# Two moves in the last jobs of the first feed-forward: the parameters' copy ahead of the fifth job's settling, and one modulation transfer behind the next weights

## The chip, the cores and the metric

The kernel runs on one core of a Trainium2 chip. The metric is the device time of one execution in microseconds, the median of the runs shown.

## The reference

The kernel computes one inference step of a trunk with two layers. Each layer has two feed-forwards around a set of token mixers:

```python
def trunk_layer(x, mod, p, ctx):
    shift, scale, gate = mod[:, :, :, 0], mod[:, :, :, 1], mod[:, :, :, 2]
    h = modulate(x, shift[:, :, 0], scale[:, :, 0])
    x = layer_norm(ALPHA * x + 0.5 * gate[:, :, 0] * swiglu(h, p['ffn_w_gu'][0], p['ffn_w_down'][0]),
                   p['ln_g'][0], p['ln_b'][0])
    h = modulate(x, shift[:, :, 1], scale[:, :, 1])
    u, state = token_mixing(h, p, ctx)
    x = layer_norm(ALPHA * x + gate[:, :, 1] * u, p['ln_g'][1], p['ln_b'][1])
    h = modulate(x, shift[:, :, 2], scale[:, :, 2])
    x = layer_norm(ALPHA * x + 0.5 * gate[:, :, 2] * swiglu(h, p['ffn_w_gu'][1], p['ffn_w_down'][1]),
                   p['ln_g'][2], p['ln_b'][2])
    return x, state
```

where `swiglu` is `(silu(gate) * up) @ w_down` with `gate, up = split(h @ w_gu)`, and `mod` is `silu(c) @ w_mod + b_mod`, nine vectors of 1024 for each layer and each of two conditions. There are 512 latent and 128 context tokens, 640 columns in all; the model width is 1024 and the feed-forward's is 2816. The token mixers are four (latent attention, a state-space scan, a gated linear scan, windowed attention), computed from one input projection; their small parameters (norm weights, convolution taps, biases, skip and sink values) are what `parameters()` prepares.

## The kernel before

Activations lie with the features on the 128 partitions and the 640 tokens along them; `X` (`x_res`) is the residual stream in eight tiles of 128 x 640. Each engine has a program of its own, written out by hand, which it runs in order; semaphores tie them together. An engine that waits holds everything behind it in its own program. SyncE (SP) issues all the transfers, in order too.

**A feed-forward** is done in two groups (`g` = 0, 1). Each group has 11 jobs of gate and up products, and then eight jobs (`m` = 0 to 7) that multiply the hidden tile by a block of `ffn_w_down` and give one tile of `X` each. The change is in the eight jobs of group 1, here called the first to the eighth (the fifth is `m == 4`). Every weight block is loaded by SP into one of two raw buffers (in `w_slots`, line 506, two transfers for a job), rounded by ScalarE (`weights_hi`, `w_split` from `w_slots`), and subtracted from the raw one by VectorE (`weights_lo`, line 1684), and TensorE multiplies in three split products (line 730). The raw buffer is free when `weights_lo` is done; the split buffers when the job that reads them is done. `weights_hi(n + 2)` and `weights_lo(n + 2)` for the job after next stand in front of a job's own work on ScalarE and VectorE, so at `m == 4` the seventh job's weights are split, and at `m == 5` the eighth's.

After a job VectorE adds the product to `X[:, m]` (line 1784, three operations, the *residual*), which frees the job's banks of PSUM (`f_freed`), and calls `settle(sub, m)`, which prepares the layer norm. At `m == 4` this is long: it waits for the mean that TensorE computes behind the fifth job (line 810), subtracts it from the first eight half-tiles (eight operations of line 1698), and adds up squares (line 1704) that ScalarE makes meanwhile, in turn with it.

**Modulation products.** The vectors of `mod` are computed in pieces of 512 in between. `mod_rows` (line 597, 64 small matmuls) needs a 2 MB block of `w_mod`, which SP loads with `fill_mod` (line 405) into `h_mod` or `mixed`; ScalarE copies the rows (`mod_copy`, into `new_rows`), TensorE turns them (`mod_turn`, line 606), and VectorE adds the bias (`mod_add`, lines 1631 to 1635). In a feed-forward's group 1, TensorE runs the product of `mods[0]` behind the fourth job and its turn behind the fifth, the product of `mods[1]` behind the sixth and its turn behind the seventh. The blocks of `mods[2]` and `mods[3]` go into the same two places, so SP waits for those two products (`mod_row`) before it issues them; they are used in the layer norm, the first by the product that follows the eighth job. The last feed-forward of all has no modulation pieces.

**Parameters.** In the first feed-forward of each layer (`sub == 0`) TensorE also transposes the mixers' parameter rows into bank 2, behind the mean at `m == 4` (line 799), and VectorE's `parameters()` copies them out (line 1674) and does four more small operations on 4 or 8 columns. The product of `mods[1]` writes to bank 2 and waits for that copy:

```python
if mods and m == 5:
    if sub == 0:
        pe.wait_ge(s["par_ready"], o["par_ready"] + 1)
    mod_piece(*mods[1], 2)
```

After the feed-forward come the layer norm and the input projection (line 845 first), whose weights SP issues behind the last modulation transfer (line 476).

Of the kernel before, what the change touches and what calls it, by code (L numbers as in the profile page):

```python
# [199 lines left out]
def trunk_kernel(nc, a, consts, const_at):  # L200
    number, loaded_at, job, units = plan_layer()
    offsets, mod_at = per_layer(loaded_at, job), mod_order()
    with ExitStack() as ctx:
# [195 lines left out]
        def _(sp):  # L399
# [3 lines left out]
            def fill_mod(l, i):  # L403
                signal, _ = mod_loads(l, i)
                sp.dma_start(MOD_AT[l, i].rearrange("p (k c) -> p k c", k=KT_M), w_mod_of(l, i)).then_inc(signal, 16)
# [61 lines left out]
            for l in range(DEPTH):  # L467
# [13 lines left out]
                def fill_ffn(sub):  # L481
                    w_dn = a["ffn_w_down"][l, sub // 2].rearrange("(k p) c -> p k c", p=P)
                    mods = [*ffn_mods(l, sub), *norm_mods(l, sub)]
                    for g in range(2):
                        n0 = sub // 2 * FFN_JOBS + g * GROUP_JOBS
                        if g == 0 and (l or sub):
                            for c in range(2):
                                if sub == 0:
                                    sp.wait_ge(s["w_lo"], o["w_lo"] + n0 + c - 1)
                                fill_raw(l, sub, (n0 + c) % 2, c * P)  # L490
                            if sub == 0:
                                sp.wait_ge(s["f_done"], o["f_done"])
                                fill_mod(l, 4)
                                fill_mod(l, 5)
                        with sp.Fori(1 if g == 0 else 0, FG // 2) as i:
                            for c in range(2):
                                sp.wait_ge(s["w_lo"], o["w_lo"] + i * 2 + (n0 + c - 1))
                                fill_raw(l, sub, (n0 + c) % 2, i * (2 * P) + (g * FG + c) * P)
                        sp.wait_ge(s["w_lo"], o["w_lo"] + n0 + FG - 2)
                        fill_raw(l, sub, (n0 + FG - 1) % 2, (g * FG + FG - 1) * P)  # L500
                        for m in range(KT_M):
                            n = n0 + FG + m
                            sp.wait_ge(s["w_lo"], o["w_lo"] + n - 1)
                            dst = WRAW[n % 2][:, 0:FG * P].rearrange("p (k c) -> p k c", k=FG)
                            for k0, k1 in ((0, 6), (6, FG)):
                                sp.dma_start(dst[:, k0:k1], w_dn[:, g * FG + k0:g * FG + k1, m * P:(m + 1) * P])\
                                    .then_inc(raw_loaded[n % 2], 16)
                            if g == 1 and mods:
                                if m == 2:
                                    sp.wait_ge(s["f_done"], o["f_done"] + n0 + FG)  # L510
                                    fill_mod(*mods[0])
                                elif m == 3:
                                    fill_mod(*mods[1])
                                elif m == 5:
                                    sp.wait_ge(mod_row, mod_at[mods[0]] + 1)
                                    fill_mod(*mods[2])
                                elif m == 7:
                                    sp.wait_ge(mod_row, mod_at[mods[1]] + 1)
                                    fill_mod(*mods[3])
# [1099 lines left out]
        def _(dve):  # L1619
# [45 lines left out]
            for l in range(DEPTH):  # L1665
# [78 lines left out]
                def ffn(sub):  # L1744
# [11 lines left out]
                    for g in range(2):  # L1756
# [17 lines left out]
                        for m in range(KT_M):  # L1774
                            n = n0 + FG + m
                            if n + 2 < (sub // 2 + 1) * FFN_JOBS or sub == 2 and l + 1 < DEPTH and m == 6:
                                weights_lo(n + 2)
                            if m == 0:
                                dve.wait_ge(mod_done, mod_at[l, 6 * sub + 5] + 1)
                            dve.wait_ge(s["f_done"], o["f_done"] + n + 1)  # L1780
                            b = 4 * (n % 2)
                            for src, t0, cols, grp in ((banks[:, b, 0:HALF], 0, HALF, 0), (banks[:, b + 1, 0:LAT - HALF], HALF, LAT - HALF, 0),
                                                       (banks[:, b + 1, LAT - HALF:HALF], LAT, CTX, 1)):
                                ins = v.scalar_tensor_tensor(out=X[:, m, t0:t0 + cols], in0=src, scalar=MOD[:, sub, 2, m, grp:grp + 1],
                                                             in1=X[:, m, t0:t0 + cols], op0=ALU.mult, op1=ALU.add)
                            ins.then_inc(f_freed[n % 2], 1)
                            if g == 1:
                                dve.wait_ge(f_freed[n % 2], o["f_freed"][n % 2] + n // 2 + 1)
                                settle(sub, m)
                                mods = ffn_mods(l, sub)  # L1790
                                if mods and m in (4, 6):
                                    mod_add(*mods[m // 5], 3)
                                if sub == 0 and m == 4:
                                    parameters()

                def layer_norm(sub, meanwhile=None):
                    mods = norm_mods(l, sub)
# [210 lines left out]
                for lev in range(1, LEVELS + 1):  # L2008
                    m = 2 ** (lev - 1)
# [191 lines left out]
```

## Time and profile before

| | |
|---|---|
| median of 3 runs | 3230.68 us |
| lowest, highest | 3225.84, 3233.95 us |
| the profiled execution | 3226.51 us |
| its span | 3224.7 us |
| TensorE busy (matmul) | 2998.4 us, 93% |
| VectorE busy | 1254.8 us, 39% |
| ScalarE busy | 913.7 us, 28% |
| mean granted TensorE clock | 0.963 of full speed |
| DMA | 259.02 MB, mean 80 GB/s |

The span is from the first to the last instruction of the profiled execution; its time lies 1.8 us above that. A share of busy time is an average over stages with different limits. TensorE is named PE in the rows, its weight loads PEld, VectorE DVE, ScalarE ACT, SyncE's queue SPq.

### The profile page before, as it was taken

How to read it: one execution, taken by the hardware profiler on the slowest of the kernel's cores; microseconds unless marked ns; L12 is line 12 of the kernel's file. 1: busy time of each engine (PE TensorE's matmuls, PEld its weight loads, DVE VectorE, ACT ScalarE, POOL GpSimd, SP SyncE). 2: the span in 40 equal slices, each digit the busy share in tenths (PEclk: the TensorE clock that was granted, in tenths of full speed). 3: DMA queues.
4: the chain of work that ended last, by engine and by line, in shares of the span. 5: the costliest groups of instructions: out<-in, count | busy, mean ns of one | idle time of the engine just before them, and what ended most of it. 6: DMA issues, size and time to landing. Idle time of an engine off the chain costs nothing.

```text
span 3224.7 us, 46427 instructions
## 1 busy us (share of the span) xinstructions
PE 2998.4 (93%) x20149; PEld 2647.7 (82%) x20149; DVE 1254.8 (39%) x1639; ACT 913.7 (28%) x1270; POOL 144.9 (4%) x88
## 2 busy tenths in 40 slices
PE   6999998997789999999979999989978998999997
PEld 6999997775556589999979999967655665999996
DVE  3223236435443442322542322464363426223226
ACT  3222223322344132222242121233223433221223
POOL 0000000105200000000000000000150000000000
PEclk8999999999889999999989999999987999999998
DMA  8223233104220122222532232421142001223221
GB/s 295 66 67 84 78 106 115 53 27 131 79 86 1 40 78 66 80 78 73 164 106 69 72 83 70 133 71 53 53 157 83 29 1 50 81 59 90 68 67 51
DMA packets 359016, 259.02 MB, mean 80 GB/s; under 512 B 27152, under 2 KB 310100, under 8 KB 358740
## 3 DMA queue, kind: packets, MB, share of 16 engines
q1 hardware_dynamic: 358868, 256.85, 26.4%
q8 instruction: 117, 1.92, 0.3%
q14 instruction: 31, 0.25, 0.0%
HBM read 253.25 MB, written 3.57 MB: 80 GB/s over the span
## 4 chain that ended last, share of the span: by engine, by line
PE 85%; DVE 7%; ACT 3%; DMA 2%; issue 1%; SPq 1%; POOL 0%; DVEq 0%; ACTq 0%; PEldq 0%; POOLq 0%
PE banks L730 54%; PE banks L646 17%; ACT arena L1248 2%; PE banks L597 2%; PE banks L1165 2%; PE banks L845 1%; PE banks L1186 1%; DVE x_res L1805 1%; PE banks L1016 1%; DMA w_slots<-in_w_mod 1%; PE banks L1158 1%; DMA w_slots<-in_ffn_w_down 1%; DVE w_split L1684 1%; PE banks L911 1%; PE banks L896 1%
## 5 line engine op out<-in xcount | busy, mean ns | idle before, releaser
L730 PE MATMUL banks<-h_hi,w_split 128*128 128x320 f32 x5376 | 1184.5, 309 | 1.0 <-DVE mod L1633 1.0
L730 PEld LDWEIGHTS banks<-h_hi,w_split 128*128 128x128 f32 x5376 | 899.2, 188 | 1.4 <-issue 1.4
L730 PE MATMUL banks<-h_lo,w_split 128*128 128x320 f32 x2688 | 830.6, 309 | 0.0
L730 PE MATMUL banks<-hid_hi,w_split 128*128 128x320 f32 x2816 | 625.1, 310 | 0.1
L1684 DVE TENSOR_TENSOR w_split<-w_slots,w_split 128x2048 fp32r<-128x2048 f32 x152 | 348.4, 2292 | 424.0 <-ACT w_split L1248 423.9
L730 PEld LDWEIGHTS banks<-h_lo,w_split 128*128 128x128 f32 x2688 | 504.6, 188 | 0.0
L1248 ACT ACTIVATE arena<-banks 128x640 f32<-128x640 f32 (+8 forms) x336 | 169.4, 535 | 1082.0 <-PE banks L730 804.2
L730 PEld LDWEIGHTS banks<-hid_hi,w_split 128*128 128x128 f32 x2816 | 472.8, 188 | 2.0 <-issue 1.6
L730 PE MATMUL banks<-hid_lo,w_split 128*128 128x320 f32 x1408 | 435.5, 309 | 0.0
L1248 ACT ACTIVATE w_split<-w_slots 128x2048 fp32r<-128x2048 f32 x152 | 290.1, 1909 | 407.2 <-PE banks L730 371.2
L1748 DVE TENSOR_TENSOR arena<-arena,banks 128x640 f32<-128x640 f32 x88 | 72.2, 821 | 767.5 <-ACT arena L1248 767.5
L646 PE MATMUL banks<-h_mod,w_slots 128*128 128x320 f32 (+3 forms) x1024 | 287.4, 440 | 2.7 <-DMA w_slots<-in_w_in 2.0
L646 PEld LDWEIGHTS banks<-h_mod,w_slots 128*128 128x128 f32 (+1 forms) x1024 | 183.0, 192 | 101.4 <-issue 44.6
L730 PEld LDWEIGHTS banks<-hid_lo,w_split 128*128 128x128 f32 x1408 | 264.8, 188 | 0.0
L646 PE MATMUL banks<-mixed,w_slots 128*128 128x128 f32 (+1 forms) x512 | 144.1, 443 | 1.6 <-DVE mixed L2110 1.0
L646 PEld LDWEIGHTS banks<-mixed,w_slots 128*128 128x128 f32 x512 | 79.4, 194 | 66.6 <-issue 64.7
L1248 ACT ACT_TABLE_LOAD x72 | 92.4, 1283 | 122.6 <-PE banks L730 88.1
L2170 POOL TENSOR_TENSOR arena<-arena 128x640 f32<-128x640 f32 x56 | 109.6, 1958 | 82.5 <-ACT arena L1248 79.2
L2082 DVE TENSOR_REDUCE softmax_cols<-banks 128x1 f32<-128x640 f32 (+3 forms) x80 | 51.0, 637 | 115.2 <-PE banks L1165 67.9
L646 PEld LDWEIGHTS banks<-arena 128*128 128x128 f32 x560 | 68.7, 193 | 27.3 <-ACT arena L1248 26.7
L1248 ACT ACTIVATE arena<-arena 128x640 f32<-128x640 f32 (+4 forms) x87 | 64.6, 795 | 92.2 <-DVEq L2053 47.7
L2138 POOL MEMSET arena<- 128x4 f32 (+1 forms) x6 | 6.0, 996 | 1869.3 <-ACT h_mod L1248 1869.1
(260 smaller groups left out, 2643.1 us busy)
## 6 DMA issues: line engine op xcount, KB each, us to landing
w_slots<-in_ffn_w_gu SPq DMA_DIRECT2D x176, 512.0 KB, 5.1
w_slots<-in_ffn_w_down SPq DMA_DIRECT2D x64, 384.0 KB, 3.7
w_slots<-in_w_mod SPq DMA_DIRECT2D x12, 2048.0 KB, 7.9
arena<-in_w_mod SPq DMA_DIRECT2D x10, 2048.0 KB, 12.9
w_slots<-in_ffn_w_down SPq DMA_DIRECT2D x64, 320.0 KB, 4.3
h_mod<-in_w_mod SPq DMA_DIRECT2D x8, 2048.0 KB, 8.1
mixed<-in_w_mod SPq DMA_DIRECT2D x6, 2048.0 KB, 9.7
w_slots<-in_w_in SPq DMA_DIRECT2D x6, 2048.0 KB, 8.4
```

Of the source, the lines that this page charges most:

```text
L597: ins = mm(banks[N_TURN * q:N_TURN * (q + 1), bank, turned_cols(n)], SC[:, k, :], w[:, k, q, :], start=k == 0, stop=k == KT_M - 1, skip_gr ...
L646: ins = mm(out, lhs, rhs, start=i == 0, stop=i == len(pairs) - 1)
L730: ins = mm(banks[:, b0 + hf, 0:HALF], w[:, k, :], x[:, k, t], start=w is wlo and k == 0, stop=w is whi and x is hi and k == kt - 1, skip_g ...
L845: ins = mm(p_cols(f"x{ct}", b), w_zx[:, k, 256 + ct * P:256 + (ct + 1) * P], H[:, k, t0:t0 + n], start=k == 0, stop=k == KT_M - 1, skip_gr ...
L896: ins = mm(banks[:, 4 + c % 2, :], past[:, d], STEP[:, c % 2, d], start=d == 0, stop=d == 1)
L911: ins = mm(banks[:, 6 + c % 2, 256 + h * 64:320 + h * 64], SCORE[:, c % 2, d, h * P:(h + 1) * P], XDT[:, d, c, h * 64:(h + 1) * 64], start ...
L1165: ins = mm(flat[:, 0:n], q, key[:, un["lo"] * P:un["hi"] * P], start=True, stop=not masked, skip_group_check=True)
L1248: return nc.scalar.activation(out, in_, func, **kw)
L1684: v.tensor_tensor(WLO[n % 2], WRAW[n % 2], WHI[n % 2].bitcast(F32), ALU.subtract).then_inc(s["w_lo"], 1)
L1748: v.tensor_tensor(GATE[:, c].rearrange("p (h t) -> p h t", h=2), GATE[:, c].rearrange("p (h t) -> p h t", h=2), banks[:, 4 * par + 2:4 * p ...
L2082: link(v.reduce_max(sc[:, 0:1], src, AX_X))
L2170: g.tensor_tensor(dst, dst, wide(add), ALU.add).then_inc(s["sums"], 1)
```

## The change

VectorE's call of `parameters()` moves from behind the fifth job's settling and `mod_add` to in front of the settling. SyncE issues the transfer of `mods[2]` behind the seventh job's weights and no longer behind the sixth's. The first holds for the first feed-forward of both layers, the second for all three feed-forwards that have modulation pieces.

```diff
@@ fill_ffn, SyncE @@
                                 elif m == 3:
                                     fill_mod(*mods[1])
-                                elif m == 5:
+                                elif m == 6:
                                     sp.wait_ge(mod_row, mod_at[mods[0]] + 1)
                                     fill_mod(*mods[2])
                                 elif m == 7:
@@ ffn, VectorE @@
                             if g == 1:
                                 dve.wait_ge(f_freed[n % 2], o["f_freed"][n % 2] + n // 2 + 1)
+                                if sub == 0 and m == 4:
+                                    parameters()
                                 settle(sub, m)
                                 mods = ffn_mods(l, sub)
                                 if mods and m in (4, 6):
                                     mod_add(*mods[m // 5], 3)
-                                if sub == 0 and m == 4:
-                                    parameters()
```

No instruction is added or taken away on any engine, and the programs of TensorE, ScalarE and GpSimd are the same. VectorE's program in layer 0, before, from the last of the fifth job's sums of squares (the settling's end) to the sixth job's residual:

```order
L1704 TENSOR_TENSOR arena<-arena,h_mod 128x640 [waits squared,sq_added]
L1635 TENSOR_TENSOR mod<-banks,par_0 128x8 [waits mod_turned,sq_added]
L1674 COPY par<-banks 128x31 [waits par_turned]
L1675 TENSOR_SCALAR one_minus_lb<-lb 128x4 [waits par_ready]
L1676 TENSOR_SCALAR sink<-sink 128x4 [waits dve_chain]
L1677 TENSOR_TENSOR skip<-skip_par 128x4 [waits dve_chain]
L1679 TENSOR_SCALAR dt_par<-dt_par 128x8 [waits dt_step,skip_ready]
L1684 TENSOR_TENSOR w_split<-w_slots,w_split 128x2048 [waits w_hi,dve_chain]
L1784 SCALAR_TENSOR_TENSOR x_res<-banks,mod,x_res 128x320 [waits f_done]
```

And of the change, from the fifth job's residual to the settling's first operations:

```order
L1784 SCALAR_TENSOR_TENSOR x_res<-banks,mod,x_res 128x128
L1674 COPY par<-banks 128x31 [waits par_turned,ffn_freed_even]
L1675 TENSOR_SCALAR one_minus_lb<-lb 128x4 [waits par_ready]
L1676 TENSOR_SCALAR sink<-sink 128x4 [waits dve_chain]
L1677 TENSOR_TENSOR skip<-skip_par 128x4 [waits dve_chain]
L1679 TENSOR_SCALAR dt_par<-dt_par 128x8 [waits dt_step,skip_ready]
L1698 SCALAR_TENSOR_TENSOR x_res<-banks,x_res 128x2x512 [waits mean_ready,dve_chain]
L1698 SCALAR_TENSOR_TENSOR x_res<-banks,x_res 128x2x128
```

The five operations stood behind the settling's twelve and the bias addition of line 1635; now they stand before all of these, and the split of line 1684 follows the bias addition.

SyncE's program in layer 0, the difference at the sixth and seventh jobs (each job's weights are two rows of line 506, and the row of line 405 is the transfer of `mods[2]`):

```order
 L506 DMA w_slots<-in_ffn_w_down 128x6x128 [waits w_lo]
 L506 DMA w_slots<-in_ffn_w_down 128x5x128
+L506 DMA w_slots<-in_ffn_w_down 128x6x128 [waits w_lo]
+L506 DMA w_slots<-in_ffn_w_down 128x5x128
 L405 DMA h_mod<-in_w_mod 128x8x512 [waits mod_row]
-L506 DMA w_slots<-in_ffn_w_down 128x6x128 [waits w_lo]
-L506 DMA w_slots<-in_ffn_w_down 128x5x128
```

The seventh job's two transfers now stand ahead of the modulation transfer and its wait, and the eighth's follow it.

## Rows read from the trace of the kernel before

**Rows 1.** The page, part 4: chain that ended last, shares of the span by line.
```profile
PE banks L730 54%; PE banks L646 17%; ACT arena L1248 2%; PE banks L597 2%; PE banks L1165 2%; PE banks L845 1%; PE banks L1186 1%; DVE x_res L1805 1%; PE banks L1016 1%; DMA w_slots<-in_w_mod 1%; PE banks L1158 1%; DMA w_slots<-in_ffn_w_down 1%; DVE w_split L1684 1%; PE banks L911 1%; PE banks L896 1%
```
**Rows 2.** TensorE's waits, whole span: us in total, times, longest.
```profile
PE banks L597 <- DVE par L1674: 13.1, 2, 7.2
```
**Rows 3.** The chain in layer 0: start, us, what.
```profile
484.60 0.58 SPq L506
...
485.22 9.50 DMA w_slots<-in_ffn_w_down
...
548.21 11.98 PE banks L845 x33
```
**Rows 4.** TensorE's timeline: start, us, operation, [idle before]; layer 0, control, layer 1.
```profile
504.93 0.31 PE L730 MATMUL banks<-hid_hi,w_split 128*128 128x320 f32 x1
511.17 3.64 PE L597 MATMUL banks<-mixed,cond 128*32 128x128 f32 x64 [5.93 <-DVE par L1674]
...
535.17 1.95 PE L597 MATMUL banks<-h_mod,cond 128*32 128x128 f32 x64
...
1587.85 0.31 PE L730 MATMUL banks<-hid_hi,w_split 128*128 128x320 f32 x1
...
1599.76 0.27 PE L606 MATMUL banks<-cst,new_rows 128*128 128x128 f32 x1
...
1609.64 0.63 PE L597 MATMUL banks<-h_mod,cond 128*32 128x128 f32 x14
...
2091.45 0.31 PE L730 MATMUL banks<-hid_hi,w_split 128*128 128x320 f32 x1
...
2122.69 0.54 PE L597 MATMUL banks<-h_mod,cond 128*32 128x128 f32 x12
```
**Rows 5.** VectorE's timeline, layer 0 and (last row) layer 1.
```profile
474.67 2.29 DVE L1684 TENSOR_TENSOR w_split<-w_slots,w_split 128x2048 fp32r<-128x2048 f32 x1 [5.49 <-ACT w_split L1248]
...
498.96 1.13 DVE L1784 SCALAR_TENSOR_TENSOR x_res<-banks,mod,x_res 128x320 f32<-128x320 f32 x3
...
510.94 0.18 DVE L1674 COPY par<-banks 128x31 f32<-128x31 f32 x1
...
511.96 2.29 DVE L1684 TENSOR_TENSOR w_split<-w_slots,w_split 128x2048 fp32r<-128x2048 f32 x1
514.17 1.13 DVE L1784 SCALAR_TENSOR_TENSOR x_res<-banks,mod,x_res 128x320 f32<-128x320 f32 x3
...
2101.97 1.13 DVE L1784 SCALAR_TENSOR_TENSOR x_res<-banks,mod,x_res 128x320 f32<-128x320 f32 x3
```
**Rows 6.** TensorE's timeline behind the fifth job, layers 0 and 1.
```profile
493.84 0.27 PE L606 MATMUL banks<-cst,new_rows 128*128 128x128 f32 x1
...
495.12 0.24 PE L799 MATMUL banks<-cst,new_rows 31*128 31x31 f32 x1
...
2080.36 0.27 PE L606 MATMUL banks<-cst,new_rows 128*128 128x128 f32 x1
```
**Rows 7.** ScalarE's timeline, both layers, and (last row) SyncE's in layer 0.
```profile
494.74 1.91 ACT L1248 ACTIVATE w_split<-w_slots 128x2048 fp32r<-128x2048 f32 x1 [8.75 <-DMA w_slots<-in_ffn_w_down]
...
509.80 1.89 ACT L1248 ACTIVATE w_split<-w_slots 128x2048 fp32r<-128x2048 f32 x1
...
2082.53 1.91 ACT L1248 ACTIVATE w_split<-w_slots 128x2048 fp32r<-128x2048 f32 x1 [10.02 <-DMA w_slots<-in_ffn_w_down]
...
515.29 24.97 SPq L476 DMA_DIRECT2D w_slots<-in_w_in  x5
```
**Rows 8.** Windows: start:end, length, each engine's busy us; PEclk is the third from the end.
```profile
505.00:511.00 6.00, 0.24 (x2) 0.00 (x0) 4.89 (x8) 3.21 (x4) 0.00 (x0) 0.88 0.00 0
511.00:516.70 5.70, 5.53 (x72) 4.92 (x73) 5.36 (x12) 1.71 (x3) 0.00 (x0) 0.52 0.11 17
1588.00:1609.70 21.70, 21.70 (x203) 21.21 (x205) 14.21 (x19) 7.46 (x8) 0.00 (x0) 1.00 0.65 194
```
**Rows 9.** Transfers to and from `w_slots`, 460 to 545 us.
```profile
DMA to landing us min/median/max: 3.4/6.4/13.0
```

## The prediction

> **What bounds the kernel now.** The chain that ended last spends 54% of the span on TensorE's split products of line 730 and 17% on its products of line 646 [rows 1]. So time is to be had only where TensorE stands still. The list of its waits says where: 13.1 us in 2 waits, the longer 7.2, end with the copy of line 1674, the first operation of `parameters()` [rows 2]. That is one wait in each layer's first feed-forward, and the change is about it.
>
> There the chain in layer 0 runs: SyncE issues the weights of the seventh of the eight last jobs at 484.60, they land at 494.72 [rows 3], ScalarE splits them, VectorE subtracts, adds the fifth job's residual, settles (eight operations of line 1698, four of 1704), copies at 510.94 [rows 5], and only then does TensorE start at 511.17 the modulation product behind the sixth job. Its last matmul of that job had started at 504.93; between them it idles 5.93 us [rows 4]. The product writes into the PSUM bank that the copy reads, so it must wait for it.
>
> The trace also has a control. The second feed-forward of layer 0 runs the same jobs, modulation products and settling, without `parameters()`. There the sixth job's last matmul starts at 1587.85, the small transpose ("turn") behind the seventh at 1599.76, and the product behind the eighth at 1609.64 [rows 4].
>
> **Part one: the parameters in front of the settling.** Nothing is added; five small VectorE operations move from 510.94 to the end of the fifth job's residual at 500.09 (498.96 + 1.13) [rows 5]. Before, the next split follows the last of them at 511.96, so they take 1.02 us with their waits [rows 5]. What they wait for is there: the transpose that the copy reads runs on TensorE at 495.12 [rows 6], 4.7 us before the residual's end (0.24 us of it its own), and ScalarE's exponential stands ahead of the split of 494.74, whose idle time before it, 8.75 us, began when the exponential was over [rows 7]. So the copy is done about 500.3, and TensorE is free for the product at 505.2.
>
> The worth of that, by the control: from the sixth job's last matmul to the product behind the eighth it is 1609.64 - 1587.85 = 21.79 us. In layer 0 it is 535.17 - 504.93 = 30.24, in layer 1 2122.69 - 2091.45 = 31.24 [rows 4]. The differences are 8.45 and 9.45, together 17.9 us.
>
> Of these, 13.1 are idle time. The other 4.8 are TensorE's lower clock: in the idle stretch of layer 0 the granted clock falls (mean 0.88 from 505 to 511), in the 5.7 us after it the mean is 0.52, so nearly all at 1.2 GHz, and through the whole control it is 1.00, 2.4 GHz [rows 8]. The product takes 3.64 us where the one behind the eighth job takes 1.95 [rows 4].
>
> The Trainium skill, "TensorE: Matmul & The Clock Gate", in its table of terms, has a rule for this: the loss is about the gated time times one half. By [rows 8] the gated time in layer 0 is 2 x (12% of 6 + 48% of 5.7) = 6.9 us, so by the page the clock costs 3.4 us there; doubled for two layers and with the 13.1, its sum would be 20.0 us. The rule charges gated time in which TensorE had no work, which the control does not, and I keep the 17.9.
>
> **What may take the wait's place.** For the eighth job TensorE needs its split weights and the bank that the sixth job's residual frees, and in VectorE's queue settling, split and residual follow each other. Before, that residual ends at 515.30 (514.17 + 1.13), in layer 1 at 2103.10 (2101.97 + 1.13) [rows 5]. The parameters were ahead of it before and are ahead of it after, so their place moves this end by nothing. At the control's pace, 1599.76 - 1587.85 = 11.91, TensorE wants the eighth job at 516.84 and 2103.36. That is a margin of 1.5 us in layer 0 and only 0.26 in layer 1, if nothing else moves.
>
> **Part two: one transfer behind the next weights.** SyncE's queue is in order. Before, it stands at the modulation transfer until the product ahead of the fifth job is done, issues its 2 MB (128 x 4096 floats), and behind it, at 484.60, the seventh job's weights [rows 3]. These had been free to go since the split of 474.67 ended at 476.96 [rows 5]. ScalarE waits for their landing, not for TensorE: its split starts at 494.74 and 2082.53 [rows 7], while the fifth job is over at 493.84 and 2080.36, where the turn starts [rows 6]. After the change they are issued at 477 and, if they take the 10.1 us they took behind the 2 MB, are there by 487. The splits and the settling then start 0.8 and 2.1 us earlier, and the margins become 2.3 us in both layers. TensorE gains nothing more by this: it is cover for part one.
>
> The transfer itself isn't late: its last wait is still the product's end, so it goes at about 484.2 as before, for use at 535.17 [rows 4]. Behind it now stand the eighth job's weights. The seventh's stood there before and landed after 10.1 us (484.60 to 494.72) [rows 3]; so do these, issued at 487, by 497, and ScalarE wants them at 509.80 [rows 7]: 12 us of cover. The other modulation transfer, which waits for the product of part one, goes some 7.7 us earlier (511.17 + 3.64 against 505.17 + 1.95). In the second feed-forward of layer 0 the same move is made, but TensorE has no wait there before the eighth job's end: worth 0.
>
> **The sum.** 8.45 + 9.45 + 0 = 17.9 us. Against the profiled execution that is a span of 3224.7 - 17.9 = 3206.8 and a time of 3226.51 - 17.9 = 3208.6. This execution lies 4.2 under the median of the runs shown, so for the median it is 3230.68 - 17.9 = 3212.8, which I predict. What follows, layer norm and projection, is released by the eighth job's end and moves with it.
>
> **The rivals.** *The forecast*, chance 0.82: both waits and their low clock vanish; 3212.8.
>
> *A new wait for the eighth job*, 0.08. VectorE comes late there: the seventh's weights arrive no earlier, or the small operations take longer ahead of the settling. For it speaks the margin of 0.26 us in layer 1; against it the 2.1 us that part two adds. It decides nothing until the row slips by more than 2.3 us; a slip 3 us beyond that in each layer costs 6, and perhaps 1 of clock: a gain of 11, 3220.
>
> *The gain is given back*, 0.07. The projection's weights might not come earlier: they are issued at 515.29, behind the eighth job's split [rows 7], and the slowest landing in this stretch took 13.0 us [rows 9], so they are there at 528.3. TensorE starts on them at 548.21 [rows 3] and would start 8.45 earlier, at 539.8, so 11 us are left. It decides if they land later than 539.8; given back in half the time is 3221.7, in whole 3230.7. That the change does nothing is this case too: TensorE would be waiting for something other than the copy. Against that, the copy ends at 511.12 (510.94 + 0.18) and TensorE starts 0.05 later [rows 4, 5].
>
> *Slower*, 0.03. `parameters()` is now ahead of the settling, and VectorE is in order: if the transpose or the exponential were late, settling, the eighth split and the sixth residual would all be held. It decides when the hold exceeds 8.45 + 2.3 = 10.8 us in a layer, that is if the transpose of 495.12 ended after 510. A hold of 16 us in each layer gives 3230.68 + 2 x 5.2 = 3241. Against it is its place in TensorE's row [rows 6].
>
> **How the numbers follow.** This kernel's measurement tells a change from none at about 0.3%, 9.7 us. The forecast, the first rival and what of the second gives back less than half lie beyond that: 0.92 faster. Same 0.06; slower 0.02, since part of that case stays inside 9.7. The range: below, 3206, from the profiled execution as the truer base (3208.6) and 2.6 for scatter and for the skill's 20.0; above, 3220, the new wait at its price. Only cases of 0.1 together lie outside.
>
> **What would show it.** The copy of 1674 no longer among TensorE's waits and starting within 0.3 us of the fifth job's residual; the product behind the sixth job 1.95 us long, within 0.3 us of that job's end, at a granted clock of 1.00; 21.8 us from the sixth job's last matmul to the product behind the eighth, in both layers; ScalarE's split for the seventh job released by TensorE in all three feed-forwards that have modulation transfers. The forecast is wrong if TensorE waits for lines 1684 or 1784 before the eighth job, or for the projection's weights, or if the clock falls in these stretches all the same.

## The result and the profile after

| | before | changed |
|---|---|---|
| median, six runs each | 3228.26 us (3221.0 to 3233.95) | 3204.44 us (3201.63 to 3207.67) |
| the profiled execution, its span | 3226.51, 3224.7 us | 3204.47, 3202.7 us |
| ratio, 95% interval | | 0.9927 (0.9911 to 0.9942) |

The change makes the kernel faster, by the ratios some 24 us in this comparison and 20 and 23 in two later ones. The forecast of 3212.8 had the direction and both waits right; the measured time lies 1.6 us below its range.

The changed kernel's waits of TensorE in the stretch from 450 to 535 us, in full; the list from 2060 to 2110 us consists of the same one row. The wait for the copy of line 1674 [rows 2] is gone and nothing stands in its place:

```profile
PE banks L810 <- DVE arena L1726: 0.3, 1, 0.3
```

TensorE's timeline of the changed kernel, in the places of [rows 4]: the sixth job's last matmul, the product behind it, the turn, and the product behind the eighth job, in layer 0; and the first and the last of these in layer 1.

```profile
505.41 0.31 PE L730 MATMUL banks<-hid_hi,w_split 128*128 128x320 f32 x1
505.65 1.96 PE L597 MATMUL banks<-mixed,cond 128*32 128x128 f32 x64
...
517.32 0.27 PE L606 MATMUL banks<-cst,new_rows 128*128 128x128 f32 x1
...
527.21 1.95 PE L597 MATMUL banks<-h_mod,cond 128*32 128x128 f32 x64
...
2083.69 0.31 PE L730 MATMUL banks<-hid_hi,w_split 128*128 128x320 f32 x1
...
2105.48 1.95 PE L597 MATMUL banks<-h_mod,cond 128*32 128x128 f32 x64
```

The product starts 0.24 us after the last matmul of its job starts, and takes 1.96 us in place of 3.64. From that last matmul to the product behind the eighth job it is 527.21 - 505.41 = 21.80 us and 2105.48 - 2083.69 = 21.79; the control gave 21.79. The windows over these stretches, which answer to [rows 8], show the full clock:

```profile
505.60:511.40 5.80, 5.80 (x91) 5.55 (x91) 4.69 (x7) 2.73 (x4) 0.00 (x0) 1.00 0.42 134
511.40:529.00 17.60, 17.60 (x173) 17.29 (x171) 9.94 (x18) 3.29 (x5) 0.00 (x0) 1.00 0.58 201
...
2083.90:2105.50 21.60, 21.60 (x201) 21.17 (x200) 13.07 (x20) 5.55 (x7) 0.00 (x0) 1.00 0.56 196
```

VectorE's timeline, which answers to [rows 5] (the view ended at 503 us, so its row of line 1698 has three of the eight operations). The copy follows the fifth job's residual at once. The last two rows are the part that the forecast had wrong: before, the split for the eighth job followed on the parameters without a gap; now VectorE waits 0.71 us for ScalarE ahead of it.

```profile
498.80 1.13 DVE L1784 SCALAR_TENSOR_TENSOR x_res<-banks,mod,x_res 128x320 f32<-128x320 f32 x3
499.97 0.19 DVE L1674 COPY par<-banks 128x31 f32<-128x31 f32 x1
...
501.00 2.81 DVE L1698 SCALAR_TENSOR_TENSOR x_res<-banks,x_res 128x1024 f32<-128x1024 f32 x3
...
512.61 2.29 DVE L1684 TENSOR_TENSOR w_split<-w_slots,w_split 128x2048 fp32r<-128x2048 f32 x1 [0.71 <-ACT w_split L1248]
514.82 1.13 DVE L1784 SCALAR_TENSOR_TENSOR x_res<-banks,mod,x_res 128x320 f32<-128x320 f32 x3
```

ScalarE's timeline, for [rows 7]: its split for the seventh job is released by the end of the fifth job and no longer by a landing, in layer 0, in the second feed-forward of layer 0 (1569.79) and in layer 1.

```profile
494.58 1.91 ACT L1248 ACTIVATE w_split<-w_slots 128x2048 fp32r<-128x2048 f32 x1 [8.11 <-PE banks L730]
...
1569.79 1.91 ACT L1248 ACTIVATE w_split<-w_slots 128x2048 fp32r<-128x2048 f32 x1 [9.63 <-PE banks L730]
...
2072.86 1.91 ACT L1248 ACTIVATE w_split<-w_slots 128x2048 fp32r<-128x2048 f32 x1 [8.11 <-PE banks L730]
```

And SyncE's: the fifth to the seventh job's weights in one row (the last of the six transfers is issued by 478.4), the modulation transfer, the eighth's weights, and the other modulation transfer at 507.67, right behind the product's end (before, it was issued at 514.88).

```profile
458.05 20.39 SPq L506 DMA_DIRECT2D w_slots<-in_ffn_w_down  x6
484.67 0.37 SPq L405 DMA_DIRECT2D h_mod<-in_w_mod  x1
487.15 0.96 SPq L506 DMA_DIRECT2D w_slots<-in_ffn_w_down  x2
507.67 0.37 SPq L405 DMA_DIRECT2D mixed<-in_w_mod  x1
```

So the two feed-forwards gave, measured from the product ahead of the fifth job to the one behind the eighth, what was forecast for them. But the spans of the two profiled executions differ by 22.0 us. The rest, some 4 us, came later. This is what most of the experiments are about.

**How the stages are measured.** The table takes start times of VectorE's operations from the traces: *feed-forward* is from the scaling of the residual (line 1692; in layer 1 the first operation of line 1688) to the layer norm's first (line 1800); *mixers* from the first operation of line 2004 (in the gated scan) to the first of line 1738 (the output projection's residual), attention included. Each other stage agrees within 2 us among all these traces, and the kernel's start, up to the first scaling of the residual, within 3.4 us.

| kernel | feed-forward, layer 0 | layer 1 | mixers, layer 0 | layer 1 | span |
|---|---|---|---|---|---|
| before | 477.23 | 493.13 | 317.95 | 318.43 | 3224.7 |
| before_again | 476.26 | 493.13 | 314.09 | 314.61 | 3215.9 |
| before_third | 476.99 | 493.28 | 317.98 | 318.46 | 3226.1 |
| changed | 468.79 | 483.82 | 318.14 | 314.21 | 3202.7 |
| after_again | 468.80 | 483.81 | 317.34 | 314.18 | 3202.0 |
| after_third | 468.81 | 483.84 | 317.34 | 317.57 | 3205.3 |
| params_only | 468.80 | 484.32 | 317.22 | 317.35 | 3204.5 |
| dma_only | 476.90 | 490.61 | 318.21 | 317.42 | 3220.6 |
| fill_idle | 475.06 | 490.11 | 317.50 | 322.04 | 3221.2 |
| late4 | 472.44 | 485.84 | 313.98 | 314.83 | 3205.8 |
| pad24 | 468.80 | 487.28 | 317.21 | 317.49 | 3207.8 |
| pad48 | 468.93 | 490.56 | 318.28 | 331.92 | 3227.4 |
| early24 | 472.34 | 483.70 | 317.10 | 320.81 | 3209.7 |
| early57 | 477.16 | 484.00 | 318.31 | 317.75 | 3213.8 |
| pad64 | 468.80 | 493.21 | 317.21 | 318.50 | 3216.3 |
| padback | 477.17 | 493.43 | 320.96 | 314.81 | 3226.1 |

The feed-forwards of the three traces of either kernel agree within 1 us, and their means differ by 8.03 and 9.36 us, 17.4 together. The mixers, where no instruction differs in any of these kernels, run from 314.0 to 331.9 us. In the mean of the three traces of either kernel, though, both layers' mixers together differ by only 0.9 us (633.8 and 632.9) and the spans by 18.9; that the rest of the gain comes from the mixers is read from single traces, the first pair above all.

### The profile page after: what moved, and what is told of

Its sections match the earlier page's. It is cut to its first block, busy times and chain, and to the rows that moved or that the text cites. A ratio compares the mean times of both kernels' runs of the same rounds, so it can differ in the third digit from the quotient of the medians.

```text
span 3202.7 us, 46427 instructions
## 1 busy us (share of the span) xinstructions
PE 2990.8 (93%) x20149; PEld 2642.1 (82%) x20149; DVE 1254.6 (39%) x1639; ACT 913.6 (29%) x1270; POOL 144.9 (5%) x88
## 4 chain that ended last, share of the span: by engine, by line
PE 86%; DVE 6%; ACT 3%; DMA 2%; SPq 1%; issue 1%; POOL 0%; DVEq 0%; ACTq 0%; PEldq 0%; POOLq 0%
PE banks L730 55%; PE banks L646 17%; ACT arena L1248 2%; PE banks L1165 1%; PE banks L597 1%; PE banks L845 1%; DVE x_res L1805 1%; PE banks L1186 1%; PE banks L1016 1%; PE banks L1158 1%; DVE w_split L1684 1%; SPq L476 1%; PE banks L911 1%; PE banks L896 1%; PE banks L1108 1%
```

## The experiments

The theory at the start: the gain is the two waits and the low clock behind them, all of it in the two feed-forwards; what was measured beyond is scatter of the mixers' clock (theory A). The rival: the change shortens what follows too, or moves it to where it is shorter (theory B).

### The kernels themselves again

No edit: **after_again** and **after_third** are the changed kernel, **before_again** and **before_third** the kernel before.

> The changed kernel once more, for its ratio and a second trace. In the first pair of traces the two first feed-forwards gave 8.44 and 9.44 us, as the sum said (8.45 and 9.45), and 4.6 us more came between 2135 us and 3162 us of the kernel before, mostly in layer 1's mixers, where the granted clock from about 2450 to 2500 was lower in the trace of before. Theory A: this is how the clock happened to fall in that execution; with more runs the gain is near 17.9 us (ratio 0.9945, interval holding it) and the stretch of the mixers varies from trace to trace of one kernel by some us. Theory B: the change shortens the mixers too; the gain stays at 22 us or more (ratio at most 0.993) and every trace of the changed kernel has the short stretch.

> The kernel before against itself: ratio 1.000, its interval the measure of what can be told. Its trace is a second one of the same program. Theory A: layer 1's mixers differ between the two traces of before by 2 us or more with the same program; theory B: they agree within 1 us.

> The changed kernel a third time. Theory A: its trace may show a scan of layer 1 other than 133.0, up to 138 us, and the median stays near 3204.6. Theory B: 133.0 again.

> The kernel before a third time, for its third trace. The two first feed-forwards, from the start of the scaling of the residual to the layer norm, should be 17 to 18 us longer in sum than in the changed kernel's; the scans anywhere from 133 to 138 us in either layer, so that the spans of its three traces spread by some 9 us.

Measured: after_again 3204.74 us, ratio 0.9938 (0.9925 to 0.9951); after_third 3205.86, ratio 0.9928 (0.9907 to 0.9949). before_again 3226.91, ratio 1.0005 (0.9997 to 1.0014); before_third 3226.33, ratio 0.9995 (0.9980 to 1.0011).

Two things follow. First, mixers of one program differ from trace to trace: by 3.9 us between before and before_again in each layer, by 3.4 us between after_again and after_third in layer 1. In the latter pair the stage begins at 2306.53 and 2306.44 us, so even at the same time it isn't the same. The windows of the two over the same 25 us, after_again first and after_third in the fence behind it, show where it comes from, a granted clock of 0.80 against 0.66:

```profile
2415.00:2440.00 25.00, 18.82 (x125) 14.44 (x124) 9.03 (x32) 4.53 (x9) 0.00 (x0) 0.80 0.00 1
```

```profile
2415.00:2440.00 25.00, 19.27 (x104) 15.16 (x104) 8.76 (x31) 3.90 (x8) 0.00 (x0) 0.66 0.00 1
```

Second, scatter alone doesn't explain the size. Over all comparisons the kernel before has a median of 3226.0 in 112 executions, 20 of them above 3230; the changed kernel has 3205.5 in 17, none above 3207.7. That is 20.5 us, 3 more than the feed-forwards' 17.4. That the long executions have gone is likely but not shown by 17: in the comparison of after_again the kernel before, too, had 23 executions without one above 3229.0. Theory A's plain form, a gain of 17.9 with the same spread, has a point against it, and theory B's, that the short stage comes each time, has the 317.57 of after_third.

### Each part alone

**params_only** has the second hunk of the change, **dma_only** the first.

```diff
 params_only, against the kernel before
+                                if sub == 0 and m == 4:
+                                    parameters()
                                 settle(sub, m)
...
-                                if sub == 0 and m == 4:
-                                    parameters()
 dma_only, against the kernel before
-                                elif m == 5:
+                                elif m == 6:
                                     sp.wait_ge(mod_row, mod_at[mods[0]] + 1)
```

> Only the copy of the parameters is moved ahead of the settling; the modulation transfer stays in front of the seventh job's weights. By the sum the gain is all here, 17.9 us less at most 1: the residual of the sixth job ends 1.5 us (layer 0) and 0.26 us (layer 1) before TensorE wants the eighth job, so a wait there is at most a few tenths in layer 1. The rival, that part two carries some of the gain, expects a TensorE wait of 1 to 2 us before the eighth job in layer 1 and a gain of 16 or less. By theory B the gain is 22.

> Only the transfer is moved; the parameters stay behind the settling. The settling starts 0.8 us earlier in layer 0 and 2.1 us earlier in layer 1, and since TensorE here still waits for the copy behind it, its idle time falls from 5.9 to about 5.1 and from 7.2 to about 5.1: a gain of 2.9 us, perhaps 1 more if the clock falls later. The idea that this part is only worth something as cover expects 0.

params_only: 3205.82 us, ratio 0.9939 (0.9926 to 0.9951); dma_only: 3221.54, ratio 0.9991 (0.9982 to 1.0000). So the parameters alone bring what both bring, within the interval. In its trace a wait for the bank that the sixth job's residual frees has appeared in layer 1 and not in layer 0. The waits of params_only from 2060 to 2112 us:

```profile
PE banks L810 <- DVE arena L1726: 0.3, 1, 0.3
PE banks L730 <- DVE x_res L1784: 0.2, 1, 0.2
```

and its feed-forward of layer 1 is 0.5 us longer than the changed kernel's (484.32 against 483.82), about as a margin of 0.26 us less 0.8 makes it. The 0.8 is what the sixth job's residual slips against the fifth's: before, their ends are 15.21 us apart (500.09 to 515.30), in the changed kernel 16.02 (499.93 to 515.95). That is the whole worth of the cover. dma_only's gain of 2.9 us (0 to 5.8) agrees with the expected one, though its interval ends at none; the wait that both layers keep falls from 5.9 and 7.2 to 5.3 in each, here from its list of TensorE's waits:

```profile
PE banks L597 <- DVE par L1674: 10.6, 2, 5.3
```

### The price of the clock

**fill_idle** is the kernel before with matmuls in the idle time, whose result the next job overwrites.

```diff
                             if mods and m == 5:
                                 if sub == 0:
+                                    pe.wait_ge(f_freed[(n + 1) % 2], o["f_freed"][(n + 1) % 2] + (n + 1) // 2)
+                                    pe.wait_ge(s["w_lo"], o["w_lo"] + n + 2)
+                                    for _ in range(36):
+                                        mm(banks[:, 4 * ((n + 1) % 2), 0:HALF], WHI[(n + 1) % 2][:, 0:P], HIDHI[:, 0, 0:HALF],
+                                           start=True, stop=True, skip_group_check=True)
                                     pe.wait_ge(s["par_ready"], o["par_ready"] + 1)
```

> The kernel before, with 36 more matmuls of the down-projection's kind on TensorE in front of its wait for the parameters' copy, in both layers; their result goes to a bank that the next job overwrites. They take 5.3 us of the 5.9 and 7.2 us of idle time, so the wait itself stays, but TensorE is not idle. Theory (the wait costs twice, as idle time and as lower clock): granted clock 1.00 after the wait, the product 1.95 us long in place of 3.64, and a gain of 2.4 and 2.2 us, 4.6 to 4.8 together. Rival (the lower clock is not due to the idle time): the product still takes 3.64 us and the time is that of before.

3222.12 us, ratio 0.9986 (0.9976 to 0.9995): by the ratio 4.5 us faster than before, with more work. The product behind the wait, whose line is the same here, is back at its short form (TensorE's timeline of fill_idle, both layers):

```profile
511.25 1.95 PE L597 MATMUL banks<-mixed,cond 128*32 128x128 f32 x64 [0.90 <-DVE par L1679]
...
2093.84 1.95 PE L597 MATMUL banks<-mixed,cond 128*32 128x128 f32 x64 [0.71 <-DVE par L1679]
```

The feed-forwards are 1.77 us (476.83, the mean of three, less 475.06) and 3.07 us (493.18 less 490.11) shorter than before's, 4.8 together. That this is just the clock's term of the sum is partly chance, since, counted from the product ahead of the fifth job, the copy came 1.2 us earlier in layer 1 than in the trace of before (the seventh job's weights had landed sooner) and 0.2 later in layer 0. The clock alone is seen from the product's start to the start of the one behind the eighth job: 21.56 us in both layers, where before has 24.00 (535.17 less 511.17) and 23.72 (2122.69 less 2098.97), so 2.4 and 2.2 us, as expected. The rows for it, fill_idle's in both layers and, in the second fence, the product of layer 1 before:

```profile
532.80 1.95 PE L597 MATMUL banks<-h_mod,cond 128*32 128x128 f32 x64
...
2115.40 1.95 PE L597 MATMUL banks<-h_mod,cond 128*32 128x128 f32 x64
```

```profile
2098.97 3.64 PE L597 MATMUL banks<-mixed,cond 128*32 128x128 f32 x64 [7.21 <-DVE par L1674]
```

It was TensorE's standing still that made it slow.

### The margin before the eighth job

**late4** puts 3.3 us of work on VectorE between the parameters and the settling of the changed kernel.

```diff
                                 if sub == 0 and m == 4:
                                     parameters()
+                                    for _ in range(4):
+                                        link(v.tensor_tensor(GATE[:, 1], GATE[:, 1], GATE[:, 1], ALU.max))
                                 settle(sub, m)
```

> The changed kernel with four more VectorE operations (each of 128 x 640 elements, about 0.82 us, on a buffer that is overwritten later) between the parameters and the settling, 3.3 us in each layer's first feed-forward. My forecast put the margin before the eighth job at 2.3 us in both layers, which gives a TensorE wait of 1.0 us in each and 2 us more than the changed kernel. The trace of the changed kernel instead shows the sixth job's residual ending 1.37 us before the turn, since VectorE waits 0.71 us for ScalarE's split: then the wait is 1.9 us in each and the time 3.9 us more.

3209.63 us, ratio 0.9954 (0.9940 to 0.9968), 4.1 us more than the changed kernel's 3205.5. TensorE waits before the eighth job in both layers; its timeline there:

```profile
520.23 0.41 PE L730 MATMUL banks<-hid_hi,w_split 128*128 128x320 f32 x1 [1.85 <-DVE x_res L1784]
...
2096.87 0.42 PE L730 MATMUL banks<-hid_hi,w_split 128*128 128x320 f32 x1 [1.86 <-DVE x_res L1784]
```

That is 3.3 less 1.4: the margin is 1.4 us and not 2.3. The same wait cost 3.64 us in layer 0 (472.44 less 468.80) and 2.02 in layer 1; that these 5.7 us are more than the 4.1 of the median is left open by five executions from 3206.4 to 3215.7. The windows behind the two waits say why:

```profile
520.20:526.00 5.80, 5.77 (x29) 5.77 (x30) 4.60 (x8) 1.48 (x2) 0.00 (x0) 0.71 1.02 345
...
2098.00:2104.00 6.00, 6.00 (x43) 6.00 (x42) 3.61 (x7) 0.74 (x1) 0.00 (x0) 1.00 0.83 314
```

After 1.85 us of idle time the clock fell for part of the next 6 us in one layer and stayed whole in the other. A short wait may cost its own length or nearly twice that. The mixers have many such waits: in layer 1 of the changed kernel TensorE is busy for 268 of 314 us, and none of its waits there is above 4.8 us. That the same happens at them is argued from this one pair, not shown wait by wait.

### Where the later stages lie

Here the changed kernel gets more matmuls, 0.147 us each, behind the sixth job: **pad24** and **pad48** 24 and 48 in layer 1, **early24** 24 in layer 0, **early57** 57 in layer 0, **pad64** 64 in layer 1, **padback** both of the latter. They delay all that follows and leave TensorE no idle time in the wait's place. The diff is that of the last three kernels; the others have the layer and the number written out.

```diff
                                 if sub == 0:
                                     pe.wait_ge(s["par_ready"], o["par_ready"] + 1)
+                                    if l in PAD:
+                                        pe.wait_ge(f_freed[(n + 1) % 2], o["f_freed"][(n + 1) % 2] + (n + 1) // 2)
+                                        pe.wait_ge(s["w_lo"], o["w_lo"] + n + 2)
+                                        for _ in range(PAD[l]):
+                                            mm(banks[:, 4 * ((n + 1) % 2), 0:HALF], WHI[(n + 1) % 2][:, 0:P], HIDHI[:, 0, 0:HALF],
+                                               start=True, stop=True, skip_group_check=True)
```

> The changed kernel with 24 more matmuls (3.5 us, 0.147 us each) on TensorE behind the sixth job in layer 1 only, so that layer 1's mixers come 3.5 us later after layer 0's; nothing else moves. Theory A (the gated scan's length varies with how the clock falls in an execution, whatever the change): the changed kernel's median plus 3.5 us, 3208.2, and the scan of either layer (from the first operation of line 2004 to the first of 2051) somewhere between 133 and 137 us. Theory B (the distance between the two layers sets how the clock falls in the second scan): the sum is off by 2 us or more, and layer 1's scan differs from the 133.0 of both traces of the changed kernel.

> The same with 48 matmuls, 7.0 us. Theory A: 3211.7, with a scan anywhere from 133 to 137 us. Theory B: off by 2 us or more, in another direction or size than with 24.

> The changed kernel with the 24 more matmuls behind the sixth job in layer 0 only, 3.5 us, so that both layers' mixers come later by the same and their distance stays that of the changed kernel. Theory A (the scans' lengths scatter by execution): 3204.6 + 3.5 = 3208.1, the scans between 133 and 138 us. Theory B (the distance between the layers decides the second scan): also 3208.1, but layer 1's scan is again 133.0 us, as in both traces of the changed kernel, where the same 24 matmuls in layer 1 gave 7.5 us more in the median and a scan of 136.2.

> The changed kernel with 57 more matmuls behind the sixth job in layer 0 and 64 in layer 1, 8.4 and 9.4 us at 0.147 us each: TensorE is busy where the kernel before stands idle or slow, and everything behind it comes as late as there. Theory A (the change is worth the 17.4 to 17.9 us of the two feed-forwards, and what was measured beyond is scatter): 3204.9 + 17.8 = 3222.7, with the narrow spread of the changed kernel. Theory B (the time of what follows, above all of the gated scans, depends on when it comes; the changed kernel happens to lie well, the kernel before not): the time of the kernel before, 3226, and its wide spread (above 3230 in some executions).

> Only layer 0's 57 matmuls, 8.4 us. Theory A: 3213.3. Theory B: 2 us or more beside it, or the wide spread.

> Only layer 1's 64 matmuls, 9.4 us. Theory A: 3214.3. Theory B: 2 us or more beside it; layer 1's alone gave 4 and 3 us too much with 24 and 48 matmuls.

Measured, beside the changed kernel's median of all 17 executions, 3205.5, plus what the feed-forwards with the added matmuls grew by in the table:

| kernel | feed-forwards longer by | 3205.5 plus that | measured median | beyond |
|---|---|---|---|---|
| early24 | 3.5 | 3209.0 | 3210.29 | 1.3 |
| pad24 | 3.5 | 3209.0 | 3212.18 | 3.2 |
| pad48 | 6.7 | 3212.2 | 3214.62 | 2.4 |
| early57 | 8.4 | 3213.9 | 3219.51 | 5.6 |
| pad64 | 9.4 | 3214.9 | 3219.23 | 4.3 |
| padback | 18.0 | 3223.5 | 3227.90 | 4.4 |

(early57 had one execution of 6963 us among its 12, which I can't explain; the median isn't moved by it.) The ratios to the kernel before are 0.9943 (0.9922 to 0.9964), 0.9956 (0.9943 to 0.9970), 0.9962 (0.9948 to 0.9976), 0.9981 (0.9965 to 0.9998), 0.9984 (0.9970 to 0.9998) and, for padback, 1.0000 (0.9987 to 1.0013).

padback is the plainest of them. It has no wait for the copy, its two feed-forwards are as long as those of the kernel before (477.17 and 493.43 against 477.2 and 493.1), and its median is 3227.90 where the kernel before has 3226.0 beside it, not the 3222.7 of theory A. The interval of its ratio reaches down to 0.9987 (3221.8) and wouldn't exclude 3222.7 by itself; but none of its 12 executions is below 3225.6. Its spread, 3225.6 to 3231.4, is the narrow one of theory A, not the wide one of theory B. The changed kernel wasn't run beside padback, early57 and pad64; the kernel before has the same median there as over all, so the sums hold to about 1 us. The medians of all six pads lie above their sums, by 1.3 to 5.6 us, the 1.3 of early24 and, with five executions, the 3.2 of pad24 within the scatter. So some 3 to 4 us of the change's gain come back with the old position. Theory A is refuted as far as the medians go.

Three things stay open. Position and stage length aren't tied one to one in single traces: padback's mixers of layer 1 begin within 6 us of those of before and have the short mixers, 314.81; its trace is 22.8 us longer than the mean of the changed kernel's three, 18.0 in the feed-forwards, 2.8 in the mixers and 2.0 in the start, ahead of the first feed-forward, which no position can explain. early24 leaves the distance between the layers as in the changed kernel, to 1 us, and yet has a layer 1 of 320.81, so theory B's form of it, that the distance sets the length, has fallen too. And a rival wasn't tested: that the added matmuls themselves, and not the later position, slow what follows. Against it stands fill_idle, which has 36 of them in each layer and gained what was expected. Why the changed kernel's position is a good one isn't settled by these runs.

Where the time goes can be seen, at its worst, in pad48's profiled execution (3229.19 us, 14.6 above its median): its mixers of layer 1 take 331.92, and the windows over the whole stage show a mean granted clock of 0.85 (first fence), where the changed kernel's, with the same work, has 0.90 (second fence).

```profile
2313.90:2645.80 331.90, 282.70 (x1844) 189.69 (x1843) 147.26 (x248) 114.77 (x242) 56.81 (x30) 0.85 0.21 69
```

```profile
2307.20:2621.40 314.20, 268.20 (x1845) 182.70 (x1843) 146.40 (x248) 115.09 (x242) 56.87 (x30) 0.90 0.22 73
```

TensorE is busy 14.5 us longer with the same matmuls, of the stage's 17.7; VectorE, ScalarE and GpSimd are as busy as in the other within 1 us. The other 3 us are longer waits: those for the modulation transfers (line 597) add up to 17.8 us where the changed kernel has 13.8.

### A version that goes further

**warm** is the changed kernel with matmuls of constants where TensorE stands idle ahead of three feed-forwards.

```diff
+FILL = {(0, 2): 8, (1, 0): 22, (1, 2): 8}
...
+                                if c == 0 and (l or sub):
+                                    for _ in range(FILL[l, sub]):
+                                        mm(banks[:, 4 * (n0 % 2), 0:HALF], ones, cst[:, 0:HALF],
+                                           start=True, stop=True, skip_group_check=True)
...
                         mod_piece(*mods[1], rows_bank)
+                        if sub:
+                            for _ in range(6):
+                                mm(banks[:, 0, 0:HALF], ones, cst[:, 0:HALF], start=True, stop=True, skip_group_check=True)
                         mod_turn(*mods[1], 3)
```

> The changed kernel with more matmuls of constants (128 x 320, float32, about 0.53 us at full clock) where TensorE stands idle ahead of a feed-forward: 6 in the 3.65 us before the last turn of a layer norm and then 8 or 22 before the first job, in the three places where TensorE is idle 9 to 17 us and works at half the clock for 5.3 us after. Nothing waits for them. If idle time costs clock here as it did in the sixth job's wait: the granted clock stays at 1.00, the first job's 5.3 us of slow matmuls take 2.6 us less at the place where nothing else limits it (layer 1's first feed-forward), and 0 to 2 less at the two others, where VectorE's split of the input paces the first job: 3 to 5 us in all, 3200 to 3202. Rival: the first job is paced by the input's tiles at all three places and the gain is under 1 us.

3203.19 us, ratio 0.9920 (0.9899 to 0.9941), against 3205.86 and 0.9928 for the changed kernel on the same chip: the best median of all, but not told apart from the changed kernel by the intervals. Layer 1's first feed-forward, up to the copy, is 1.9 us shorter (450.97 us in the trace of warm, 452.86 in after_third). The gain at the other two places didn't come: the second feed-forward of layer 0 is 1.4 us longer than in after_third (482.80 us instead of 481.38) and that of layer 1 the same within 0.2. In the former the fillers themselves ran slowly (granted clock 0.64 from 1121.5 to 1125 us), and the first job starts 2.3 us after the time of after_third (1127.36 and 1125.02), behind the last of them. So the forecast of 3 to 5 us was too high.

## Why the prediction was right, and where it was wrong

- **The waits and the control.** Right to 0.01 us: from the product ahead of the fifth job (482.17 before, 482.65 after) to the one behind the eighth it is 53.00 and 44.56 us, 8.44 less; in layer 1 (2068.70 and 2060.93) 53.99 and 44.55, 9.44 less. A second execution of the same jobs without the disputed operation, in the same trace, priced idle time and clock together. Over three traces each it is 8.03 and 9.36; in before_again the product of layer 0 takes 3.39 us in place of 3.64, so the clock's part varies.
- **Idle and clock.** 13.1 and 4.8 was right; fill_idle measured the second alone, 2.4 and 2.2 from product to product and 4.5 by the ratio. The Trainium skill's rule ("TensorE: Matmul & The Clock Gate", table of terms: gated time times one half) would have given 3.4 us for each layer and 20.0 for these stages; the trace of fill_idle disagrees with its 2.4 and 2.2, and 17.4 to 17.9 were measured there, as [rows 4] said. That its 20.0 is near the total is accident: the rest came from another place.
- **Part two.** Right in kind, cover and no gain of its own. Wrong in the margin: "The parameters were ahead of it before and are ahead of it after, so their place moves this end by nothing." Before, they ran beside ScalarE's split of the eighth job's weights, which starts when the last square is made, and cost the queue only about 0.2 us. Ahead of the settling they cost 1.02, and ScalarE's split is now what VectorE waits for, 0.71 us: the sixth residual slips by 0.8. The earlier weights gave 0.6 and 1.9 us, not 0.8 and 2.1, since ScalarE's split starts 0.26 us behind the turn even so (494.58 and 494.32). Together 1.54 + 0.64 - 0.81 = 1.37: the margin was 1.4 us, not 2.3, and without part two layer 1 would be 0.5 us longer, which params_only measured.
- **The transfers.** Right: the eighth job's weights, issued behind the modulation transfer, delay nothing, and neither does the projection. The rival of a gain given back had no share.
- **The step that failed** is the last one of the sum: "What follows, layer norm and projection, is released by the eighth job's end and moves with it." Layer norm and projection did; the mixers moved too, but the sum put their change of length at nothing, without a reason. Over 112 and 17 executions the gain is 20.5 us, of which 17.4 to 17.9 is the forecast sum. The other 3 come behind the two feed-forwards: in the first pair of traces as mixers of layer 1 that are 4.2 us shorter (318.43 and 314.21), and the median of padback, with the old position, gives them back. What makes the position good stays open.
- **The base and the range.** The larger part of the miss is another: of the 8.3 us between 3212.8 and 3204.44, 4.7 are the base, since the median of the three runs shown, 3230.68, lies so far above the 3226.0 of all executions; 2.6 are the gain beyond 17.9; and 1.0 is that the six runs lie below the changed kernel's median of 17. The range had allowed for the base, by starting from the profiled execution. Its 2.6 us below that, for scatter and for the Trainium skill's 20.0, were used up by the gain beyond the sum; the 1.0 and the 0.5 by which the profiled execution lies above the median of all did the rest. Without the gain beyond the sum the time would have been about 3207.0, inside. The kernel before's own executions reach from 3217.7 to 3242.6; that three runs can't show such a spread is the lesson for the range.

## What to carry to other kernels

Where an engine waits in one of several like stages, look for the stage of the same kind without the wait: the difference of the two prices idle time, clock and all, better than a sum of durations does. When small operations are moved on a queue, ask not only whether they stay ahead of the same instruction but what they ran beside: here they had been hidden beside another engine's split. And when TensorE's work is cut into short pieces with short waits further on, a shift in time can change what those pieces take; give the range room for it, and check a surprising gain by putting the time back with harmless work. Where three runs of a kernel spread by 8 us, their median is a poor base for a forecast: here it was 4.7 us off.

## What the runs showed of the hardware that was not expected

- An idle time of 1.85 us before the same job of the same program lowered the granted clock in one layer (mean 0.71 in the 5.8 us after it) and not in the other (1.00), in one execution.
- The same mixer code took 314.0 to 331.9 us, and two executions of one program in which it began at the same time to 0.1 us differed by 3.4 us, with a granted clock of 0.80 against 0.66 over 25 us.
- Six pads of TensorE work, 3.5 to 18 us, cost 1.3 to 5.6 us more than their own length in the medians, and the largest brought back the time of the kernel before within the interval (ratio 1.0000, 0.9987 to 1.0013).
- 5.3 us of useless matmuls in each of two waits made the kernel before 4.5 us faster.
